# Start addresses of the eight split-weight buffers of a down projection, one Trainium2 core

## The chip, the cores and the metric

The kernel runs on one core of one Trainium2 chip. The time is device microseconds of one execution. Before the change it is 2594.54 us, the median of three runs (2594.23 to 2598.03).

## The reference

Two layers over 1,024 tokens of width 1,024, each with four mixers (latent attention, a gated recurrence, stick-breaking attention, a gated linear recurrence), and behind them the feed-forward block on which this case bears:

```
h = h + mixed @ w_out[l]
u = rmsnorm(h, ln2_g[l])
h = h + (jax.nn.silu(u @ w_ffn_gate[l]) * (u @ w_ffn_up[l])) @ w_ffn_down[l]
```

The hidden width is 2,816. After the second layer comes a last RMSNorm. Everything is float32, and the result has to be as exact as float32 products.

## The kernel before, in words

TensorE multiplies in a mode that keeps only the upper part of a float32 (type F32R). To keep the precision, each operand is split into a "hi" part and a "lo" part (what hi leaves over), and every product is made of three: hi by hi, hi by lo, lo by hi, all summed in PSUM. The helper `product` (line 218) writes them: for each block of 128 contracted rows, three pairs of stationary and moving operand, each for two halves of 512 columns, so six matmuls (line 228), each with its own weight load of 128 x 128.

The feed-forward block of a layer first computes the hidden values in 22 tiles of 128 rows (`pe_product`, line 2007, with seven half-size products for a tile) and stores them to HBM. Then comes the down projection, in 11 chunks (`CHUNKS`) of 256 hidden rows. A chunk c:

- `load_down`: SyncE's queue loads two tiles of 128 x 1024 of `w_down` into `w_raw0` and `w_raw1` (`DRAW`).
- `split_down` (lines 2082 and 2085), GpSimd, for t = 0 and 1: hi from raw (times one), then lo = raw - hi. For chunk 0 they go to the general weight buffers `w_hi` and `w_lo`; for the others to one of two sets of `DSET`, set 0 for the odd chunks and set 1 for the even ones. Each set has hi0, hi1, lo0, lo1, each 128 partitions x 4,096 bytes, so eight buffers.
- `load_hidden`, `act_hidden` (line 2096, ScalarE) and `dve_hidden` (line 2102, VectorE): the same for two tiles of hidden values, which are the moving operand.
- `pe_down`: for each of eight blocks m of 128 output columns, `product` over the two tiles: 12 matmuls, so 96 for a chunk.
- `dve_down` (line 2126): VectorE adds each PSUM result into `h`.

The order is written out by hand for each engine, and semaphores join the engines. `pe_down` of chunk c waits for `down_split` (both tiles of the chunk split) and `hid_lo`; `split_down` waits for its loads, and before it overwrites a set for the matmuls that last read it: chunk 1 for product P2 of the last hidden tile, chunk 2 for all hidden products, chunk c from 3 on for the end of chunk c - 2 on TensorE. No wait looks at an address.

SBUF is laid out by hand. From each partition's first free byte there are small constants, 9,344 bytes in all, and then only buffers at multiples of 4,096 or 1,024 bytes from each other: `w_raw`, `w_hi`, `w_lo`, `rs`, `u_hi`, `u_lo`, and the region that starts at `R0`, in which `at_r(name, kb, ...)` places a buffer at `R0 + kb * 1024`. So `w_raw`, `w_hi`, `w_lo`, the hidden parts and the eight buffers of `DSET` all begin at the same remainder within 512 bytes, which is called remainder 0 here. Counted from there, the small buffers lie at others: `ones` at 352, `w_x_blocks` and `w_a_blocks` at 160, `constants` at 384. Within a weight buffer, block m starts m x 512 bytes further, which leaves the remainder as it is.

The buffers in `DSET` share their bytes with others over time: `u_b21` (at 64 KB) and the hidden stage's weights from 80 KB on before the down projection, and the squares of the next norm after it.

Of the kernel before, what the change touches and what calls it, by code (L numbers as in the profile page):

```python
# [27 lines left out]
F32R = mybir.dt.float32r  # L28
# [7 lines left out]
P = 128  # L36
D = 1024
# [43 lines left out]
def build(nc, x, positions, vec_table, w_in, w_uq, w_ukv, w_a, w_x, lb_logits, lam, w_out,  # L81
# [6 lines left out]
    with ctx:  # L88
# [35 lines left out]
        R0 = cursor[0]  # L124
        KB = 1024

        def at_u(name, kb, shape, dtype=F32):

            return nc.alloc_sbuf_tensor_at(name, shape, dtype, offset=U0 + kb * KB)

        def at_r(name, kb, shape, dtype=F32):

            return nc.alloc_sbuf_tensor_at(name, shape, dtype, offset=R0 + kb * KB)
# [948 lines left out]
        def latents(l):  # L1082
# [152 lines left out]
            def latents_dve(dve):  # L1235
# [84 lines left out]
               for j in range(2)],  # L1320
# [3 lines left out]
                                        offset=R0 + 64 * KB + 8 * (S + 8) + j * 4 * KB) for j in range(2)]]  # L1324
# [470 lines left out]
        def sum_at(i, name):  # L1795
# [12 lines left out]


        DRAW = [raw[t] for t in range(2)]  # L1810
        DSET = [[at_r(f"down{s}_{x}{t}", 64 + 16 * s + 8 * n + 4 * t, [P, D], F32R) for n, x in enumerate(("hi", "lo"))
                 for t in range(2)] for s in range(2)]
        HRAW = [at_u(f"hidden_back{t}", 16 + 4 * t, [P, S]) for t in range(2)]
        HIDH = [at_r(f"hidden_hi{b}", 16 * b, [P, 2, S], F32R) for b in range(2)]
        HIDL = [at_r(f"hidden_lo{b}", 16 * b + 8, [P, 2, S], F32R) for b in range(2)]
# [1 line left out]
        def down_weights(c):  # L1817
            if c == 0:
                return whi, wlo
            s = DSET[(c + 1) % 2]  # L1820
            return s[0:2], s[2:4]
# [801 lines left out]
```

## Time and profile before

| | us |
|---|---|
| median of three runs | 2594.54 |
| span of the profiled execution | 2596.9 |
| PE busy | 2509.6 (97%) |
| PE weight loads busy | 1985.7 (76%) |
| VectorE busy | 1656.3 (64%) |
| GpSimd busy | 974.0 (38%) |
| ScalarE busy | 949.1 (37%) |

For the profiled execution the profile gives the span alone, so no time outside it is known; it is 2.4 us above the median of the three runs and within their spread. PE is the matmuls, PEld the weight loads that run beside them; ends of matmuls are modelled, so how fast TensorE goes is read from the distance of starts, or from a stretch divided by its matmuls.

### The profile page before, as it was taken

How to read it: one execution, taken by the hardware profiler on the slowest of the kernel's cores; microseconds unless marked ns; L12 is line 12 of the kernel's file. 1: busy time of each engine (PE TensorE's matmuls, PEld its weight loads, DVE VectorE, ACT ScalarE, POOL GpSimd, SP SyncE). 2: the span in 40 equal slices, each digit the busy share in tenths (PEclk: the TensorE clock that was granted, in tenths of full speed). 3: DMA queues.
4: the chain of work that ended last, by engine and by line, in shares of the span. 5: the costliest groups of instructions: out<-in, count | busy, mean ns of one | idle time of the engine just before them, and what ended most of it. 6: DMA issues, size and time to landing. Idle time of an engine off the chain costs nothing. (4 is left out here: it accounts for less than half of the span.)

```text
span 2596.9 us, 32239 instructions
## 1 busy us (share of the span) xinstructions
PE 2509.6 (97%) x12772; PEld 1985.7 (76%) x12772; DVE 1656.3 (64%) x1765; ACT 949.1 (37%) x1380; POOL 974.0 (38%) x547
## 2 busy tenths in 40 slices
PE   7999998999999999999999999989989999999998
PEld 5777775677788888888877777666778888888887
DVE  7887359547866665655667753775586666666554
ACT  6354147533433333100244341765243333321003
POOL 2000330325646555433520014221556555644333
PEclk9999999999999999999999999999999999999999
DMA  5110210032222222522220111001322222225221
GB/s 180 33 42 9 57 29 1 1 128 84 89 75 81 90 82 74 210 98 97 98 66 9 50 33 37 17 1 58 105 73 90 81 90 82 85 87 194 97 98 66
DMA packets 208295, 193.24 MB, mean 74 GB/s; under 512 B 31249, under 2 KB 180881, under 8 KB 208146
## 3 DMA queue, kind: packets, MB, share of 16 engines
q1 hardware_dynamic: 208146, 191.17, 22.7%
q8 instruction: 103, 1.69, 0.3%
q14 instruction: 46, 0.38, 0.0%
HBM read 147.11 MB, written 44.04 MB: 74 GB/s over the span
## 5 line engine op out<-in xcount | busy, mean ns | idle before, releaser
L2126 DVE TENSOR_TENSOR h<-ps,h 128x1024 f32<-128x1024 f32 x176 | 214.8, 1223 | 197.7 <-PE ps L228 197.6
L228 PE MATMUL ps<-u_hi,w_hi 128*128 128x512 f32 x896 | 296.3, 412 | 22.3 <-PEq L166 12.7
L1971 POOL TENSOR_TENSOR w_a<-w_raw,w_a 128x512 fp32r<-128x512 f32 x110 | 177.7, 1624 | 351.0 <-ACT w_a L1961 351.0
L228 PE MATMUL ps<-u_lo,w_hi 128*128 128x512 f32 x896 | 279.9, 394 | 0.0
L228 PE MATMUL ps<-u_hi,w_lo 128*128 128x512 f32 x896 | 279.8, 394 | 0.0
L2007 PE MATMUL ps<-u_b,w_a 128*128 128x512 f32 x1056 | 253.7, 389 | 0.0
L211 POOL TENSOR_TENSOR w_hi<-w_raw,ones 128x1024 fp32r<-128x1024 f32 (+1 forms) x37 | 69.7, 1884 | 480.0 <-DMA w_raw<-w_in 227.9
L2007 PE MATMUL ps<-u_t,w_s 128*128 128x512 f32 x1056 | 247.0, 389 | 0.0
L2007 PEld LDWEIGHTS ps<-u_t,w_s 128*128 128x128 f32 x1056 | 198.0, 188 | 41.9 <-POOL w_s L1971 0.7
L2007 PEld LDWEIGHTS ps<-u_b,w_a 128*128 128x128 f32 x1056 | 198.2, 188 | 41.2
L228 PEld LDWEIGHTS ps<-u_hi,w_hi 128*128 128x128 f32 x896 | 164.3, 191 | 67.5 <-issue 33.7
L228 PEld LDWEIGHTS ps<-u_lo,w_hi 128*128 128x128 f32 x896 | 170.3, 190 | 36.9
L228 PEld LDWEIGHTS ps<-u_hi,w_lo 128*128 128x128 f32 x896 | 170.1, 190 | 36.9
L228 PE MATMUL ps<-hidden_lo,down_hi 128*128 128x512 f32 x640 | 197.1, 389 | 0.0
L228 PE MATMUL ps<-hidden_hi,down_hi 128*128 128x512 f32 x640 | 197.0, 389 | 0.0
L228 PE MATMUL ps<-hidden_hi,down_lo 128*128 128x512 f32 x640 | 197.0, 389 | 0.0
L2096 ACT ACTIVATE hidden_hi<-hidden_back 128x1024 fp32r<-128x1024 f32 x44 | 44.9, 1056 | 353.4 <-PE ps L228 305.4
L2007 PE MATMUL ps<-u_t,w_hi 128*128 128x512 f32 x528 | 166.6, 397 | 5.9 <-DVE w_sum L2044 5.9
L2082 POOL TENSOR_TENSOR down_hi<-w_raw,ones 128x1024 fp32r<-128x1024 f32 x40 | 77.8, 1945 | 248.5 <-PE ps L228 206.7
L1971 POOL TENSOR_TENSOR w_s<-w_s_raw,w_s 128x512 fp32r<-128x512 f32 x110 | 164.3, 1510 | 7.6 <-ACT w_s L1961 7.6
L2031 ACT ACTIVATE hidden_gate<-hidden_gate 128x1024 f32<-128x1024 f32 x44 | 46.8, 1063 | 263.4 <-DVE hidden_gate L2059 263.4
L228 PEld LDWEIGHTS ps<-hidden_lo,down_hi 128*128 128x128 f32 x640 | 120.1, 188 | 25.0
(378 smaller groups left out, 4901.7 us busy)
## 6 DMA issues: line engine op xcount, KB each, us to landing
w_raw<-w_gate SPq DMA_DIRECT2D x44, 512.0 KB, 3.7
w_raw<-w_up SPq DMA_DIRECT2D x44, 512.0 KB, 4.8
hidden_spill<-hidden_gate SPq DMA_DIRECT2D x44, 512.0 KB, 2.6
w_raw<-w_down SPq DMA_DIRECT2D x44, 512.0 KB, 4.5
hidden_back<-hidden_spill SPq DMA_DIRECT2D x44, 512.0 KB, 4.1
w_raw<-w_in SPq DMA_DIRECT2D x42, 512.0 KB, 3.8
h_spill<-h SPq DMA_DIRECT2D x32, 512.0 KB, 4.8
h<-h_spill SPq DMA_DIRECT2D x32, 512.0 KB, 7.0
```

What stands on the lines that cost most here:

```text
L211: nc.gpsimd.tensor_tensor(whi[i][:, 0:width], raw[i][:, 0:width], ones[:, 0:1].broadcast_to([P, width]), ALU.mult).then_inc(hi_split, 1)
L228: last = nc.tensor.matmul(ps[:, bank0 + half, :], a, b[:, half * HALF:(half + 1) * HALF], start=(k == order[0] and n == 0), stop=(k == ord ...
L1971: nc.gpsimd.tensor_tensor(lo, src, hi.bitcast(F32), ALU.subtract).then_inc(w_lo, 1)
L2007: last = nc.tensor.matmul(ps[:, bank(i, name), :], x, y, start=new and k == 0 and n == 0, stop=k == 3 and n == 2, skip_group_check=True)
L2031: nc.scalar.activation(GA[:, :], GA[:, :], ACT.Silu).then_inc(silu_done, 1)
L2082: nc.gpsimd.tensor_tensor(hi[t][:, :], DRAW[t][:, :], ones[:, 0:1].broadcast_to([P, D]), ALU.mult).then_inc(down_hi, 1)
L2096: nc.scalar.activation(HIDH[b][:, t, :], HRAW[t][:, :], ACT.Copy).then_inc(hid_hi, 1)
L2126: nc.vector.tensor_tensor(wide(h[:, m, :]), pair(p), wide(h[:, m, :]), ALU.add)\
```

## The change

The eight buffers of `DSET` are spaced by 4,608 bytes (nine times 512) in place of 4,096, and each gets a shift of its own. No other statement changes. Their remainders within 512 bytes, counted as above, are for set 0: hi0 0, hi1 32, lo0 64, lo1 128; for set 1: hi0 192, hi1 256, lo0 320, lo1 480. They took 32 KB from 64 KB on, and now take some 36 KB up to byte 36,832 + 64 KB, in front of `w1_s1` at 100 KB. The instructions of each engine, their order, shapes and waits stay as they are; only line numbers move by two and addresses differ. Each buffer still is one run of 4,096 bytes in each partition.

```diff
         DRAW = [raw[t] for t in range(2)]
-        DSET = [[at_r(f"down{s}_{x}{t}", 64 + 16 * s + 8 * n + 4 * t, [P, D], F32R) for n, x in enumerate(("hi", "lo"))
-                 for t in range(2)] for s in range(2)]
+        DOWN_SHIFT = [0, 32, 64, 128, 192, 256, 320, 480]
+        DSET = [[nc.alloc_sbuf_tensor_at(f"down{s}_{x}{t}", [P, D], F32R,
+                                         offset=R0 + 64 * KB + (4 * s + 2 * n + t) * 4608 + DOWN_SHIFT[4 * s + 2 * n + t])
+                 for n, x in enumerate(("hi", "lo")) for t in range(2)] for s in range(2)]
         HRAW = [at_u(f"hidden_back{t}", 16 + 4 * t, [P, S]) for t in range(2)]
```

## Rows read from the trace of the kernel before

**Rows 1.** Page: busy time, share of the span and instructions of each engine.

```profile
PE 2509.6 (97%) x12772; PEld 1985.7 (76%) x12772; DVE 1656.3 (64%) x1765; ACT 949.1 (37%) x1380; POOL 974.0 (38%) x547
```

**Rows 2.** Chain that ended last, second layer: start us, length us, what.

```profile
1947.89 386.53 PE ps L2007 x1704
2334.42 239.36 PE ps L228 x1056
2573.78 3.06 PE ps L2285 x28
```

**Rows 3.** Both down projections by stretch, all engines.

```profile
core 0: us, PE busy (x) PEld busy (x) DVE busy (x) ACT busy (x) POOL busy (x), PEclk, DMA share, GB/s
1061.28:1300.62 239.34, 239.34 (x1057) 198.09 (x1056) 145.52 (x117) 35.17 (x34) 109.14 (x49) 1.00 0.36 128
2334.42:2573.78 239.36, 239.36 (x1058) 198.15 (x1058) 135.16 (x112) 36.65 (x36) 99.51 (x46) 1.00 0.31 108
```

**Rows 4.** Instructions on `down_hi` and `down_lo`: duration ns min/median/max, first and last start.

```profile
L228 PEld LDWEIGHTS ps<-hidden_hi,down_hi x640: 187/188/188, 1082.9 to 2572.3; 128*128 128x128 f32 x160
L228 PEld LDWEIGHTS ps<-hidden_hi,down_lo x640: 187/188/188, 1083.8 to 2573.2; 128*128 128x128 f32 x160
L2082 POOL TENSOR_TENSOR down_hi<-w_raw,ones x40: 1888/1896/2891, 1069.8 to 2534.7; 128x1024 fp32r<-128x1024 f32 x40
L2085 POOL TENSOR_TENSOR down_lo<-w_raw,down_hi x40: 2399/2403/3281, 1071.8 to 2536.7; 128x1024 fp32r<-128x1024 f32 x40
```

**Rows 5.** Weight loads from `ones`, `w_x_blocks` and `constants`, same columns.

```profile
L1155 PEld LDWEIGHTS ps<-latent_sq,ones x24: 187/188/190, 308.1 to 1595.8; 128*128 128x128 f32 x24
L2240 PEld LDWEIGHTS ps<-group_square,ones x16: 190/190/331, 538.5 to 1815.1; 128*128 128x128 f32 x16
L705 PEld LDWEIGHTS ps<-x_conv,w_x_blocks x16: 186/190/190, 115.9 to 1492.8; 128*128 128x128 f32 x16
L694 PEld LDWEIGHTS ps<-in_gate,constants x16: 187/190/190, 112.0 to 1489.0; 128*128 128x128 f32 x16
```

**Rows 6.** Timeline of weight loads: start us, length us, engine, line, what, count.

```profile
116.47 0.19 PEld L705 LDWEIGHTS ps<-x_conv,w_x_blocks 128*128 128x128 f32 x1 [0.24 <-issue]
116.90 0.19 PEld L705 LDWEIGHTS ps<-x_conv,w_x_blocks 128*128 128x128 f32 x1 [0.24 <-issue]
...
457.73 0.19 PEld L1433 LDWEIGHTS ps<-mla_k,mla_q 96*128 96x128 f32 x1 [0.24 <-issue]
458.15 0.19 PEld L1433 LDWEIGHTS ps<-mla_k,mla_q 96*128 96x128 f32 x1 [0.24 <-issue]
...
1082.90 0.41 PEld L228 LDWEIGHTS ps<-hidden_hi,down_hi 128*128 128x128 f32 x2
1083.35 0.41 PEld L228 LDWEIGHTS ps<-hidden_lo,down_hi 128*128 128x128 f32 x2
...
2356.02 0.19 PEld L228 LDWEIGHTS ps<-hidden_hi,down_hi 128*128 128x128 f32 x1
```

**Rows 7.** Timeline of GpSimd, splits of chunk 1, first and second layer.

```profile
1069.84 1.90 POOL L2082 TENSOR_TENSOR down_hi<-w_raw,ones 128x1024 fp32r<-128x1024 f32 x1 [17.05 <-DMA w_raw<-w_down]
1071.82 2.41 POOL L2085 TENSOR_TENSOR down_lo<-w_raw,down_hi 128x1024 fp32r<-128x1024 f32 x1
1074.19 2.87 POOL L2082 TENSOR_TENSOR down_hi<-w_raw,ones 128x1024 fp32r<-128x1024 f32 x1
1077.14 3.27 POOL L2085 TENSOR_TENSOR down_lo<-w_raw,down_hi 128x1024 fp32r<-128x1024 f32 x1
...
2347.48 2.89 POOL L2082 TENSOR_TENSOR down_hi<-w_raw,ones 128x1024 fp32r<-128x1024 f32 x1
2350.45 3.28 POOL L2085 TENSOR_TENSOR down_lo<-w_raw,down_hi 128x1024 fp32r<-128x1024 f32 x1
```

**Rows 8.** Waits from 1040 to 1320 us: us in total, times, longest us.

```profile
POOL down_hi L2082 <- PE ps L228: 103.7, 8, 13.1
```

**Rows 9.** Instructions on `x_padded`, VectorE: duration ns min/median/max.

```profile
L950 DVE SCALAR_TENSOR_TENSOR x_conv<-x_padded,vectors,x_conv x12: 1283/1285/1286, 76.8 to 1455.5; 128x1024 f32<-128x1024 f32 x12
```

## The prediction

> **What bounds the kernel now.** I read the page's busy times first: TensorE is busy 97% of the span, every other engine at most 64% [rows 1]. Then the chain that ended last: in the second layer it stays on TensorE from 1947.89 us through the hidden stage and the whole down projection to 2573.78 us, with no wait in between [rows 2]. Then the two down projections as stretches: TensorE is busy in all of 239.34 us in the one and 239.36 us in the other, at the full granted clock [rows 3]. Each holds 11 chunks of 96 matmuls, 1,056. So the pace is 239.35 / 1,056 = 226.7 ns a matmul, and a chunk takes 96 x 226.7 ns = 21.76 us. In this stretch only what changes that pace, or makes TensorE wait, can change the time. Chunk 0 takes its weights from `w_hi` and `w_lo`, chunks 1 to 10 from the buffers that move.
>
> **The change part by part.** It adds, removes and moves no instruction and no wait. So no term comes from a count. What can differ is how long those instructions take that touch the eight buffers. Two engines do: GpSimd, which writes them and reads hi back, and TensorE, which reads them as weights. No DMA, no ScalarE and no VectorE instruction touches them.
>
> *TensorE.* Chunks 1 to 10 of two layers are 10 x 96 x 2 = 1,920 matmuls with 1,920 weight loads from these buffers. A load takes 187 to 188 ns [rows 4], beside the matmul before it, and the pace is 226.7 ns, so a load could grow by 226.7 - 188 = 38.7 ns before it need set the pace. The remainders that the change introduces can be looked up in other stages, since some weights already lie there at other remainders: `ones` at 352, `w_x_blocks` at 160, `constants` at 384. Their loads of the same shape take 186 to 190 ns; one kind has a single long value up to 331 ns, but its median and least value are both 190 [rows 5]. Two of these three starts are odd multiples of 32 bytes, as hi1 of set 0 (32) and lo1 of set 1 (480) will be. So from the nearest rows a load changes by -2 to +2 ns, against 38.7 ns to spare. Term: 0. Those loads belong to plain float32 matmuls and not to F32R ones, which is why I don't call it certain. From below I bound the term by the pace without any collision of reads (the first rival), from above by the 331 ns row (the second).
>
> *The streamed operand.* The hidden values keep their places, and each matmul runs through 2,048 bytes of them, four times over all remainders within 512. A load runs through exactly 512 bytes, whatever its start. So with any shift both readers still pass every remainder once or more; only their phase differs. Term: 0.
>
> *GpSimd.* A split is four operations, hi 1.9 us and lo 2.4 us twice, 8.6 us where nothing disturbs it [rows 4]. From chunk 3 on it starts as soon as TensorE leaves chunk c - 2 and has a whole chunk of 21.76 us: the 13.1 us that GpSimd waits for TensorE each time, 8 times in a layer [rows 8], is that slack. A faster GpSimd operation gains nothing. A slower one is hidden up to 2.5 times its length, except in one place: chunk 1. Its loads land late, its splits run from 1069.84 to 1077.14 + 3.27 = 1080.41 us, and TensorE's first load from them is at 1082.90 us [rows 6, 7]. That is 2.49 us of slack; in the second layer 2356.02 - (2350.45 + 3.28) = 2.29 us. That is the thinnest cover in the change. No row shows a wide GpSimd operation on another remainder. The nearest that I found is VectorE's convolution: twelve operations that read `x_padded` 4, 8 and 12 bytes past its start take 1283 to 1286 ns, the three starts alike [rows 9]. From both sides: below 0, since its gain is off the path; above, a doubling of each operation that touches an odd 32-byte start (third rival, 7.5 us). I take the value of the nearest row, 0.
>
> Sum: 0 + 0 + 0 = 0 us. Because it is a difference of nothing, it can stand on the median directly: 2594.5 us. The profiled execution's span, 2596.9 us, is 2.4 us or 0.09% above that, so the same rows would give an unchanged span too. About 0.2% (5.2 us) is what a measurement of this kernel can tell from no change.
>
> **The rivals.**
>
> *First: weight reads and streamed reads collide less, faster.* Before, weights, hidden parts and raw tiles all start at remainder 0. If both of TensorE's readers, or TensorE and another engine, got in each other's way because of that, 226.7 ns would hold a loss. 512 columns at 2.4 GHz, the level of the granted clock 1.00, are 213.3 ns at one column a cycle. The plain float32 matmuls of 512 columns start 0.43 us apart [rows 6]; if such a matmul goes over its columns twice, half of it, 215 ns, is an estimate of the pace without collisions. The gain would be up to 1,920 x (226.7 - 215) = 22 us, so 2572 us. Against it: the float32 pace is 0.43 us where the weights lie at 160 and the streamed operand at 0 (`w_x_blocks`, `x_conv`), and 0.42 us where both are at 0 (`mla_q`, `mla_k`) [rows 6]: equal remainders cost nothing there. And the 11 to 13 ns look like the price of a change of weights at every matmul, since the hidden stage has nearly the same pace: 386.53 us / 1,704 = 226.8 ns [rows 2], with other buffers. Chance 0.05.
>
> The Trainium skill bears on this rival. "TensorE: Matmul & The Clock Gate" (section "Step-by-step: what each phase is for") gives TensorE two independent read ports in SBUF, one for the streamed operand and one for weight loads; by that no collision exists to remove, and 0 stands. The same page's "Back-to-back issue gap" puts the distance of matmuls of 512 columns at about 215.8 ns when isolated, by which, as an estimate, at most 1,920 x 10.9 ns = 21 us would be there to gain; this trace shows 226.7 ns in both stages. "SBUF — State Buffer" ("A bandwidth-pool intuition that's wrong (but worth ruling out)") says contention is structural, at ports, and not a sharing of the memory; that both F32R stages go at one pace agrees.
>
> *Second: weight loads from odd 32-byte starts are slow in F32R, slower.* hi1 of set 0 serves 32 of a chunk's 96 matmuls in five chunks, lo1 of set 1 serves 16 in five: (160 + 80) x 2 layers = 480 matmuls. It decides once a load is over 226.7 ns. With the longest load that the rows have, 331 ns, each costs 331 - 226.7 = 104 ns, so 50 us: 2645 us. Against it stand the medians of 188 and 190 ns at 160 and 352. Chance 0.03.
>
> *Third: GpSimd is slow at such a start and chunk 1 is late, slower.* In chunk 1 the third operation writes hi1 of set 0 and the fourth reads it. Doubled, they take 2.87 + 3.27 = 6.14 us more in the first layer and 2.89 + 3.28 = 6.17 us in the second. Less the slack, TensorE waits 3.65 + 3.88 = 7.5 us: 2602 us, 0.3% slower. It begins to show once a layer's splits are 2.3 us longer and passes 0.2% at about (4.8 + 5.2) / 2 = 5 us more per layer. All later chunks hide even this, for 13.1 us are to spare. For it: GpSimd's rows have no other start. Against it: the whole split must grow by half. Chance 0.04.
>
> That the change does nothing at all, because shifts cancel or addresses are rounded, would give the same time as my forecast and is part of it.
>
> **How the numbers follow.** No change 0.88; first rival 0.05; second 0.03; third 0.04. So faster 0.05, same 0.88, slower 0.07. The predicted time is the median, 2594.5 us. The unchanged case by itself reaches from some 3 us below the median to the highest of the three runs, 2598.0, and 1 to 2 us beyond for another set of runs or for a small wait in chunk 1 (a split 3 us longer waits 0.5 + 0.7 us). I give 2591.5 to 2600. The two large rivals lie outside, at 0.08 together.
>
> **What the profile of the changed kernel would show.** If I am right, each down projection is again about 239.3 us for 1,056 matmuls, the loads from `down_hi` and `down_lo` have medians of 187 to 190 ns with no second value for some buffers, and the median splits are about 1.90 and 2.40 us. If the first rival holds, the stretches shrink towards 228 us while the hidden stage keeps 226.8 ns. If the second does, the loads' largest value rises over 226 ns and odd and even chunks differ in length. If the third does, splits have a second, longer level and a wait of TensorE for GpSimd appears at about 1083 and 2356 us and nowhere else. The forecast is wrong if either stretch differs by over 2.5 us, or if the time moves by over 5.2 us for a reason elsewhere.

## The result, and the profile after

The changed kernel takes 2607.58 us (median of four runs, 2606.08 to 2607.79), the one before 2595.19 us beside it: ratio 1.0044, interval 1.0031 to 1.0056. Forecast was 2594.5 us and no change. A second comparison (last experiment) gave 2604.52 to 2596.29 us, ratio 1.0033, interval 1.0021 to 1.0045. So the layout makes the kernel 0.3 to 0.4% slower, and not one of the three rivals does it as I priced them.

The two stretches of the down projection, all engines, in the changed kernel (columns as in [rows 3]):

```profile
1060.44:1304.50 244.06, 244.06 (x1057) 198.12 (x1056) 146.04 (x118) 35.28 (x34) 109.84 (x49) 1.00 0.35 125
2337.88:2581.93 244.05, 244.05 (x1059) 198.18 (x1058) 135.19 (x112) 36.64 (x36) 99.86 (x46) 1.00 0.30 106
```

Against [rows 3] each is 4.7 us longer, with as many matmuls, no wait of TensorE, and a granted clock of 1.00 as before. 2 x 4.7 = 9.4 us is more than the whole difference of the spans (2605.8 - 2596.9 = 8.9 us). The second layer by chunk, TensorE alone (window, length, busy time, rows, granted clock, DMA share, GB/s), before and then after. The first window is chunk 0, whose weights lie where they did, the second is chunk 1, and the last one after is chunk 9:

```profile
2334.26:2356.01 21.75, 21.75 (x97) 1.00 0.88 328
2356.01:2377.78 21.77, 21.77 (x98) 1.00 0.50 179
```

```profile
2337.72:2359.48 21.76, 21.76 (x97) 1.00 0.82 315
2359.48:2381.71 22.23, 22.23 (x98) 1.00 0.53 189
...
2537.32:2559.55 22.23, 22.23 (x98) 1.00 0.01 1
```

Chunk 0 keeps 21.76 us. Every other chunk takes 22.23 us, or 22.23 / 96 = 231.6 ns a matmul in place of 226.7. Chunk 9 (last row), with the DMA engines idle, is as slow as chunk 1, and so is chunk 10 (22.22 us), beside which no split of weights runs any more. So the cost does not hang on transfers or on GpSimd's writes. The instructions on `down_hi` that answer to [rows 4] (min/median/max in ns), one row of before and then three of the changed kernel:

```profile
L228 PE MATMUL ps<-hidden_hi,down_hi x640: 389/389/389, 1083.1 to 2572.5; 128*128 128x512 f32 x160
```

```profile
L228 PEld LDWEIGHTS ps<-hidden_hi,down_hi x640: 187/188/189, 1082.1 to 2580.4; 128*128 128x128 f32 x160
L228 PE MATMUL ps<-hidden_hi,down_hi x640: 387/393/398, 1082.3 to 2580.6; 128*128 128x512 f32 x160
L2084 POOL TENSOR_TENSOR down_hi<-w_raw,ones x40: 1891/1895/2896, 1070.1 to 2542.0; 128x1024 fp32r<-128x1024 f32 x40
```

Weight loads still show 188 ns and splits 1.9 us. Only the matmuls changed: their rows, whose ends are modelled, went from one value of 389 ns to a spread of 387 to 398, and their starts moved apart. The timeline of TensorE at the step into chunk 1:

```profile
1082.35 0.62 PE L228 MATMUL ps<-hidden_hi,down_hi 128*128 128x512 f32 x2
1082.80 0.61 PE L228 MATMUL ps<-hidden_lo,down_hi 128*128 128x512 f32 x2
1083.25 0.63 PE L228 MATMUL ps<-hidden_hi,down_lo 128*128 128x512 f32 x2
1083.72 0.63 PE L228 MATMUL ps<-hidden_hi,down_hi 128*128 128x512 f32 x2
```

Pairs start 0.45 us apart up to 1083.25, and the next one 0.47 us after it: hi0 of this set has shift 0, and 1083.25 is the first pair with weights from a moved buffer, lo0 at 64. Below, "pace" is the mean distance of starts of a chunk's 96 matmuls in the second layer's trace.

### The profile page after: what moved, and what is told of

It is laid out like the page before. It is cut to its first block and busy times, and to the rows that moved or that the text cites. A ratio compares the mean times of both kernels' runs of the same rounds, so it can differ in the third digit from the quotient of the medians.

```text
span 2605.8 us, 32239 instructions
## 1 busy us (share of the span) xinstructions
PE 2518.2 (97%) x12772; PEld 1984.6 (76%) x12772; DVE 1656.2 (64%) x1765; ACT 949.0 (36%) x1380; POOL 975.8 (37%) x547
## 5 line engine op out<-in xcount | busy, mean ns | idle before, releaser
L228 PE MATMUL ps<-u_hi,w_hi 128*128 128x512 f32 x896 | 295.1, 411 | 21.9 <-PEq L166 12.7
L228 PEld LDWEIGHTS ps<-hidden_hi,down_hi 128*128 128x128 f32 x640 | 120.2, 188 | 28.7
```

Of the source, the lines that this page charges most:

```text
L228: last = nc.tensor.matmul(ps[:, bank0 + half, :], a, b[:, half * HALF:(half + 1) * HALF], start=(k == order[0] and n == 0), stop=(k == ord ...
```

## The experiments

"Distance" is the remainder of the weights minus that of the streamed operand, within 256 bytes.

**One shift per chunk.** Each chunk gets its own four allocations in the space of its set, so one trace holds ten shifts, each in both layers.

```diff
+        DOWN_SHIFT = [[32, 32, 32, 32], [64, 64, 64, 64], ... [480, 480, 480, 480]]
+        DSET = [[nc.alloc_sbuf_tensor_at(f"down{c}_{x}{t}", [P, D + 8], F32R,
+                                         offset=R0 + 64 * KB + (4 * ((c + 1) % 2) + 2 * n + t) * 4608
+                                         + DOWN_SHIFT[c - 1][2 * n + t] // 32 * 32)
+                 [:, DOWN_SHIFT[c - 1][2 * n + t] % 32 // 4:DOWN_SHIFT[c - 1][2 * n + t] % 32 // 4 + D]
+                 for n, x in enumerate(("hi", "lo")) for t in range(2)] for c in range(1, 11)]
...
-            s = DSET[(c + 1) % 2]
+            s = DSET[c - 1]
```

A buffer is allocated at the multiple of 32 bytes below its shift, eight elements wider, and used from the rest of the shift on.

> All four buffers of a chunk share one shift, and each chunk from 1 to 10 has another one: 32, 64, 96, 128, 160, 192, 256, 320, 448, 480 bytes. Theory A (the distance in remainder between the weights and the streamed hidden operand decides): the chunks have different paces, at least some clearly over 226.7 ns, the same in both layers; a chunk takes 96 x its pace. Theory B (it is the unlike starts of successive weight loads within a chunk that break a fixed rhythm): all ten chunks stay at 226.7 ns, 21.76 us each, and the time stays within 2 us of before. Theory C (odd multiples of 32 bytes are slow): only chunks 1, 3 and 5 (32, 96, 160) and chunk 10 (480) are above 226.7 ns.

Chunks 2, 6, 7 and 9 of the second layer (shifts 64, 192, 256, 448), TensorE alone:

```profile
2380.74:2403.14 22.40, 22.40 (x98) 1.00 0.26 94
...
2470.34:2492.33 21.99, 21.99 (x98) 1.00 0.27 96
2492.33:2514.11 21.78, 21.78 (x98) 1.00 0.28 97
...
2536.51:2558.49 21.98, 21.98 (x97) 1.00 0.01 1
```

A uniform shift of 64 costs as much as unlike ones, and 256 costs nothing: theory A holds, B (unlike starts alone) falls, and so does C, since 64 and 320 are slow (22.40 us each). The kernel took 2605.93 us in its one run.

**Finer shifts, and more of them.** Three more sweeps with other lists in the same place:

> As the sweep before, with shifts 0, 4, 8, 16, 24, 48, 224, 288, 352, 416 bytes for chunks 1 to 10. Chunk 1 (shift 0) should be at 226.7 ns by every theory. Theory A: the small shifts tell how fine the effect is: if it goes by lines of 16 or 64 bytes, chunks 2 and 3 (4, 8 bytes) stay at 226.7 ns. Theory B: all ten chunks at 226.7 ns. Theory C: all those that are not at a multiple of 64 bytes are slower, chunks 2 to 7 and others alike.

> Uniform shift per chunk again: 12, 20, 40, 80, 104, 144, 184, 200, 216, 232 bytes for chunks 1 to 10. What is open is whether any distance is better than 0, where all kernels so far have 226.7 ns. If the cost is a collision of two periodic reads with period 256, one value may come near 213 to 216 ns; if 0 is the best, all are between 226.7 and 234.2.

> The rest of the sweep, around the low values at 192 and 0 (256): 236, 244, 248, 112, 120, 188, 196, 204, 212, 228 bytes for chunks 1 to 10. Same question: none below 226.7 ns if distance 0 is the best. Near 256 the pace should fall towards 226.7 (244, 248), near 192 towards 229.0.

They took 2607.05, 2606.64 and 2607.81 us in one run each. All paces, with five from the next experiment, by distance in bytes (a value that was tried at two or more shifts 256 apart is marked *):

| distance: ns | | | | |
|---|---|---|---|---|
| 0*: 226.8 | 4: 232.3 | 8: 230.7 | 12: 226.7 | 16: 233.3 |
| 20: 233.3 | 24: 230.1 | 32*: 233.3 to 234.4 | 40: 233.3 | 48: 233.4 |
| 64*: 233.3 | 80: 232.0 | 96*: 234.2 | 104: 233.3 | 112: 233.3 |
| 120: 226.7 | 128: 232.4 | 136: 233.3 | 144: 233.3 | 160*: 233.3 |
| 176: 230.1 | 184: 232.1 | 188: 233.2 | 192*: 229.0 | 196: 233.4 |
| 200: 230.8 | 204: 235.0 | 208: 231.9 | 212: 236.5 | 216: 232.1 |
| 224*: 233.3 | 228: 230.7 | 232: 231.1 | 236: 231.6 | 240: 228.3 |
| 244: 233.2 | 248: 233.3 | 252: 233.2 | | |

At shift 32 the second layer's chunk 1 has 234.4 and the first layer's 233.2 ns; all other values agree between layers and between shifts 256 apart within 0.1 ns. One of the best chunks and the worst, 120 and then 212 bytes in the same sweep:

```profile
2448.79:2470.56 21.77, 21.77 (x98) 1.00 0.29 97
...
2537.91:2560.61 22.70, 22.70 (x97) 1.00 0.01 1
```

None of the 37 other distances tried is better than 0: 12, 120 and 0 share 226.7 ns, and 17 of the other 35 have 233.2 to 233.4 in at least one of their chunks. So the sweep points to no version that beats the kernel before; the multiples of 4 in between were not tried. The fine structure is not monotone (4 costs 5.6 ns, 12 nothing), so "within one line of 16 or 64 bytes it is free" is false too. The last expectation also missed: the pace does not fall towards 0 and 192. It is 233.2 and 233.3 ns at 244 and 248, and 233.2 and 233.4 at 188 and 196, 4 bytes on either side of 192's 229.0, and two values, 235.0 and 236.5, lie above the 234.2 that I had as the upper end.

**Move the streamed operand.** The hidden parts of the odd chunks go to space further back in the region from `U0` on, with shifts of their own. The lo parts move as the hi parts do. For chunk 1 the writing of these parts has to wait for the last hidden product; TensorE shows no wait from it.

```diff
+        HIDDEN_SHIFT = [0, 64, 0, 32, 0, 64, 0, 64, 0, 128, 0]
+        HIDH = [nc.alloc_sbuf_tensor_at(f"hidden_hi{c}", [P, 2, S], F32R,
+                                        offset=U0 + 32 * KB + HIDDEN_SHIFT[c] if c % 2 else R0) for c in range(11)]
...
-                    act.wait_ge(p_done, product_at(TILES - 1, ("P1", "P5")[c]))
+                    act.wait_ge(p_done, (product_at(TILES - 1, "P1"), 7 * TILES)[c])
```

> In the odd chunks the hidden parts (the streamed operand) lie elsewhere and get shifts of their own. Weights / hidden, in bytes: chunk 1: 64/64, chunk 3: 32/32, chunk 5: 0/64, chunk 7: 192/64, chunk 9: 64/128. Theory A (distance between weights and streamed operand): chunks 1 and 3 are back at 226.7 ns; chunk 5 (distance -64, that is 192) at 229.0; chunk 7 (128) at 232.4; chunk 9 (-64) at 229.0. If instead the weights' own remainder decides, or their distance to w_raw and h: chunk 1 and 3 at 233.3, chunk 5 at 226.7. Even chunks go on with the sweep, weights at 208, 240, 252, 136, 176 for chunks 2, 4, 6, 8, 10: by the sweeps so far each between 226.7 and 234.2.

Odd chunks: 227.1, 227.2, 229.1, 232.4, 229.0 ns, as theory A had it to 0.5 ns. Chunk 1 (weights 64, hidden 64) and chunk 7 (192 and 64), TensorE alone:

```profile
2357.14:2378.95 21.81, 21.81 (x98) 1.00 0.51 190
...
2489.32:2511.63 22.31, 22.31 (x97) 1.00 0.30 95
```

Weights at 64 are slow against hidden parts at 0 and fast against hidden parts at 64. The even chunks gave the five values in the table, between 228.3 and 233.3 ns. It is the distance of TensorE's two operands that decides, not the weights' own place, and not their distance to `w_raw` and `h`, which stayed. The run took 2603.18 us.

**Everything 64 bytes further.**

```diff
+        cursor[0] += 64
         raw = [fixed(f"w_raw{i}", [P, 1024]) for i in range(2)]
```

> The kernel before with 64 bytes left free ahead of w_raw0, so that raw tiles, hi and lo weights, hidden parts and everything in both regions begin 64 bytes further, all at one remainder as before. Theories A and B: nothing changes, 226.7 ns everywhere, time as before within 4 us. A theory by which the absolute remainder decides: all stages of three products have another pace, up to 5 ns x some 9,000 matmuls = 45 us more.

2598.86 us in one run, beside before's 2593.1 to 2598.29 us; the second down projection from the chain of waits:

```profile
2334.23 239.36 PE ps L229 x1056
```

As [rows 2]: the absolute remainder plays no part at this shift, and a time of 3 us above the median of before is far from the 45 us of the theory that gives it one.

**All eight buffers at 64.**

```diff
+        DOWN_SHIFT = [64, 64, 64, 64, 64, 64, 64, 64]
```

> The changed kernel with one shift, 64 bytes, for all eight buffers (spacing 4608 as there). Theory A: the stretch of each down projection changes by 1,920/2 times what chunk shift 64 shows in the sweep, somewhere between 0 and +10 us in all. Theory B: both stretches at 239.35 us, the time as before, 0.0% +- 0.1%.

2609.24 us against 2595.79 us, ratio 1.0050, interval 1.0036 to 1.0064. Chunks 1 to 10 take 22.40 us each, so 1,920 x 6.6 ns = 12.7 us is what the trace says, within the interval (9.3 to 16.6 us). Theory A gave "0 to +10 us", because of a slip: it halved the 1,920 matmuls. Eight like remainders are worse (233.3 ns) than the change's eight unlike ones (231.6 ns), so unlikeness is not what makes the change slow.

**Only multiples of 256.**

```diff
+        DOWN_SHIFT = [0, 256, 0, 256, 256, 0, 256, 0]
```

> The changed kernel's spacing of 4608 bytes with shifts 0, 256, 0, 256, 256, 0, 256, 0: two remainders within 512, one within 256. Theory A with period 256: both stretches 239.4 us, the time as before, 0.0% +- 0.15%. If the period were 512 or the spacing mattered: half of the loads at another distance, some 5 to 9 us slower.

2596.96 us against 2595.69 us, ratio 1.0001, interval 0.9993 to 1.0010, and each chunk at 21.76 us. Neither the wider spacing nor the new places in SBUF cost anything. With the seven distances that repeat 256 bytes further in the sweeps, and 128 at 232.4 ns against 226.7 at 0, the period is 256.

**Which buffers of a chunk are off.**

> Which buffers of a chunk are off. hi0, hi1, lo0, lo1 in bytes, chunks 1 to 10: 64 0 0 0; 0 64 0 0; 0 0 64 0; 0 0 0 64; 0 0 64 64; 64 64 0 0; 0 256 0 256; 64 0 64 0; 0 32 64 128 (set 0 of the changed kernel); 192 256 320 480 (set 1 of it). Theory A, each load paying for its own distance: the excess over 226.7 ns is the share of loads moved times 6.6 ns: 1/3, 1/3, 1/6, 1/6, 1/3, 2/3, 0, 1/2 of it, so 228.9, 228.9, 227.8, 227.8, 228.9, 231.1, 226.7, 230.0; and 231.6, 231.5 for the last two as in the changed kernel, where the sum of the sweep's values (0, 6.5, 6.6, 5.7 by 1/3, 1/3, 1/6, 1/6) gives only 230.9, and for set 1 (2.3, 0.2, 6.6, 6.6) 229.7. If the change of distance between loads costs by itself, the first cases are above these values.

Measured, in that order: 231.1, 230.9, 230.1, 229.7, 231.1, 232.2, 226.9, 232.2 ns, then 231.5 and 231.5. The run took 2604.79 us. The last two reproduce the changed kernel in a strange neighbourhood, so the effect is local to a chunk. But the excess is not the sum of shares: one buffer of four at 64 costs 3.0 to 4.4 ns where its share would be 1.1 to 2.2. In chunk 1, which has only hi0 off, the 12 distances between starts of a block repeat as 235.7, 231.0, 235.7, 229.3, 230.7, 231.0, 235.6, 228.4, 232.6, 230.7, 226.7, 226.0 ns: these are means over seven of the chunk's eight blocks, and matmuls whose next load is from an unmoved buffer are late too. So a matmul's lateness does not hang on the distance of its own operands and its next load alone; the expectation's last case, that a change of distance between loads costs by itself, came out for shifts of 64, while the mix of 0 and 256 has 226.9 ns and so costs next to nothing. How the lateness is carried on, no run here shows. It is why shares from the sweep, 230.9 and 229.7 ns, fall short of the changed kernel's 231.6.

**Other stages.**

```diff
+        cursor[0] += 192
         RS = fixed("rs", [P, S])
```

> The kernel before with 192 bytes left free behind w_lo1, so that the weight buffers w_hi and w_lo stay where they are and everything behind them (u_hi, u_lo, both regions) begins 192 bytes further. The distance weights minus streamed operand becomes -192, that is 64 within 256, in all stages that take weights from w_hi and w_lo: input and output projections, chunk 0 of the down projections, and a quarter or so of the hidden stage. Theory A: those go at 233.3 ns (chunk 0: 22.4 us in place of 21.76), chunks 1 to 10 stay at 226.7 ns; some 4,270 matmuls x 6.6 ns = up to 28 us slower, 0.8 to 1.2%. If the effect is one of the down projection's buffers alone (their place, GpSimd's writes beside them): chunk 0 and the time stay.

2622.05 us against 2595.69 us, ratio 1.0097, interval 1.0081 to 1.0112: 26 us of the 28. From the chain of waits, one row of the kernel before and two of this one, and then chunks 0 and 2 of this one's second layer, TensorE alone:

```profile
1837.05 65.56 PE ps L228 x288
```

```profile
1858.01 67.45 PE ps L229 x288
...
1970.03 390.52 PE ps L2008 x1704
```

```profile
2360.39:2382.78 22.39, 22.39 (x97) 1.00 0.84 310
...
2404.57:2426.33 21.76, 21.76 (x97) 1.00 0.29 97
```

These 288 matmuls of the output projection had 65.56 us in the kernel before and now have 67.45, or 6.6 ns more each. The hidden stage's 1,704 had 386.53 [rows 2] and have 390.52; only its weights in `w_hi` and `w_lo` changed their distance. Chunk 0 goes to 233.3 ns, and chunks from 2 on, whose two operands moved together, stay at 226.7. So it is a property of TensorE's F32R matmuls in this kernel, not of these buffers.

**Plain float32.** The sweep 32 to 480 again, with both operands of `pe_down` read by `.bitcast(F32)`.

> The first sweep (32, 64, 96, 128, 160, 192, 256, 320, 448, 480 bytes for chunks 1 to 10) with the down projection's operands read as plain float32 and not as F32R; the products are the same or more exact. A chunk takes about 96 x 430 ns = 41.3 us, so the whole about 430 us more. Theory A as I used the rows of ones and w_x_blocks: plain float32 matmuls do not feel the distance, and all chunks have one pace within 1 ns; that would explain why those rows showed nothing. If they feel it too, the chunks differ as in F32R, and the rows misled for another reason (too few loads in a row).

3929.10 us, 1,333 us more and not 430: a plain float32 matmul stands as two rows in the trace, 429.2 ns each, so it takes 858 ns, and a chunk 82.40 us. Chunk 1 (shift 32), TensorE alone:

```profile
3079.63:3162.03 82.40, 82.40 (x193) 1.00 0.03 13
```

All ten shifted chunks have this same length. Plain float32 does not feel the distance, at any of ten shifts, seven of which are at 232 to 234 ns in F32R. But the type is not all that differs: each row has its own weight load of 190 ns, so a load comes once in 429.2 ns and not once in 226.7. Whether the type or the longer time between loads makes it blind, this run does not tell.

**The changed kernel again.**

> The changed kernel once more, in more rounds. Its first comparison gave 12.4 us between medians, while the pace of its matmuls explains 1,920 x 4.9 ns = 9.4 us. If the pace is all, the medians of more runs differ by 9.4 us (ratio 1.0036, within 0.08%), and runs of like mean granted clock by that too. If something else costs 3 us, it stays at 12 to 13 us (ratio 1.0047).

2604.52 us (six runs) against 2596.29 us, ratio 1.0033, interval 1.0021 to 1.0045: 8.2 us, and 9.4 us (1.0036) lies in it, as in the first interval. Runs of one kernel vary by 5 to 6 us, the longer ones at a lower mean granted clock. At like mean clock (five values from 0.989 to 0.993) the change is 8.2 to 9.6 us above before, as the expectation had it for a pace that is all. All runs of the change together have median 2606.1 us (ten), those of before beside the timed experiments 2595.8 us (34): 10.2 us. The 12.4 us of the first comparison needed no second cause.

## Why the prediction was wrong

- **What bounds the kernel, and that only the pace or a wait of TensorE can move it: right.** The loss is in those two stretches, 4.7 us each, at a full clock, and over the 2.5 us that I had named as the sign of being wrong.
- **The term "TensorE": the value was wrong, 0 for +9.4 us.** I asked what the loads take and found 188 ns with 38.7 ns to spare. Loads still show 188 ns. The cost came with neither a longer load row nor a load outlasting its cover: the matmuls themselves spread.
- **The step that failed is "The streamed operand"**: since both readers pass all remainders whatever the start, "only their phase differs. Term: 0". That difference is what decides, and it was worth +9.4 us. Moving either operand alone costs, moving both together costs nothing, with a period of 256 bytes. The Trainium skill's two independent read ports ("TensorE: Matmul & The Clock Gate", "Step-by-step: what each phase is for") had spoken for my term and against the first rival; the runs show a pace that depends on how the two operands lie to each other, so here the two reads are not independent in time, and the measurement decides.
- **The rows of other stages were the wrong witnesses.** `ones`, `w_x_blocks` and `constants` lie at other remainders, but their matmuls are plain float32, which the last sweep shows to be blind to the distance. I named the difference of type and passed over it, as I did over the time between their loads. All F32R matmuls of the kernel before have distance 0, so its trace held no row on this at all, and that its two F32R stages went at one pace was no sign of anything; the bounds should have been wide.
- **The first rival had the mechanism and the wrong sign.** It took equal remainders for the bad case. They are one of the best (226.7 ns at 0, 12 and 120), and none of the 37 distances tried from 4 to 252 bytes is below. Its floor of 215 ns was taken from a wrong reading: 430 ns is half of a plain float32 matmul, not a whole one that goes twice over its columns. No F32R chunk in any run came near 215 ns.
- **Second rival: no.** The longest load of the changed kernel's down projections is 189 ns, odd and even chunks are alike, and shifts 64 and 320 are as slow as 32 and 480.
- **Third rival: no.** Splits stayed at 1.90 and 2.41 us, and TensorE enters chunk 1 without a wait. The slack of chunk 1 was read rightly but never used. Nor is there anything in GpSimd's rows at odd 32-byte starts.
- **The range** left out 0.08 for two large cases. The true one, an unknown effect on 1,920 matmuls that no row bounded, was not among them; a few ns on each is 10 us.

What stays open is the mechanism inside. That the pace of these F32R matmuls depends on the distance between weights and streamed operand, with a period of 256 bytes, is shown. That it is the load of the next weights that meets the stream of the running matmul is likely, since the two run side by side, but not shown. Which parts of the memory meet, why 12 and 120 are free and 4 is not, and why plain float32 is blind, no run here tells.

## What to carry to other kernels

In a stream of F32R matmuls with a weight load each, keep the weights' and the streamed operand's start equal modulo 256 bytes; padding that is harmless for space cost 3% of the pace at 17 of the distances tried, and 4% at the worst. This is shown for one shape, 128 x 128 by 512 columns. When a change touches addresses alone, look for rows of the same type and the same pair of operands at another distance, and if there are none, say that the trace can't bound it. A sweep with another value per loop round gives ten points in one trace.

## What the runs showed of the hardware that was not expected

- A chunk of 96 F32R matmuls (128 x 128 by 512 columns, a weight load each, granted clock 1.00) goes at 226.7 to 236.5 ns a matmul by the distance of its two operands in SBUF alone; the pattern repeats within 0.1 ns between layers and between shifts 256 bytes apart, with one exception of 1.1 ns at shift 32.
- The row of a weight load has a median of 187 to 189 ns in every chunk of the sweeps, and the longest is 193 ns, all the while: its length does not tell whether it is in the way.
- A plain float32 matmul of the same size is two rows of 429.2 ns, 858 ns in all, and has the same pace at all ten shifts tried, with one weight load in 429.2 ns.
